# Expert weights loaded as pairs: one transfer of 2 MB instead of two of 1 MB, in a two-layer encoder with a top-2-of-8 expert layer

## The reference, cut to what matters

```python
def moe_swiglu(h, w_router, w_gate, w_up, w_down):
    logits = (h @ w_router).astype(jnp.float32)
    top_vals, top_idx = lax.top_k(logits, TOP_K)
    ...
    for e in range(N_EXPERTS):
        y = y + combine[..., e:e + 1] * swiglu(h, w_gate[e], w_up[e], w_down[e])
    return y
```

## Time and profile before

| | us |
|---|---|
| median of 3 runs | 1521.4 (1521.32 to 1521.8) |
| the profiled execution, its own time | 1522.17 |
| its span, first to last instruction | 1520.2 |
| TensorE busy in the span | 1500.5 |
| VectorE busy | 1190.6 |
| ScalarE busy | 1012.3 |
| granted TensorE clock, share of full speed | 0.999 |

### The profile page before, as it was taken

The page is one execution under the profiler, slowest core; times in us unless marked ns, Lnnn a source line. Parts: engine busy times, 40 slices in busy tenths (PEclk is TensorE's granted clock), DMA queues, the critical chain, the costliest instruction groups (busy, mean ns, idle before and its releaser), DMA issues.

```text
span 1520.2 us, 17780 instructions
## 1 busy us (share of the span) xinstructions
PE 1500.5 (99%) x7138; PEld 1248.9 (82%) x7138; DVE 1190.6 (78%) x960; ACT 1012.3 (67%) x971; POOL 52.5 (3%) x63
## 2 busy tenths in 40 slices
PE   9999999999999999999999999999999999999997
PEld 7888788888888888888888888888888888888885
DVE  5756755556566769899888888889889889899896
ACT  6555544435465577777777777777777777777774
POOL 1000000000000036000000000000000000000100
PEclk9999999999999999999999999999999999999999
DMA  9832555545642549999999999999999999999992
GB/s 350 337 124 91 187 194 193 180 152 173 205 163 91 172 167 424 407 347 415 372 363 400 376 374 384 392 374 372 392 380 368 391 377 373 397 365 368 420 402 92
DMA packets 96487, 460.03 MB, mean 303 GB/s; under 512 B 7656, under 2 KB 13304, under 8 KB 53392
## 3 DMA queue, kind: packets, MB, share of 16 engines
q1 hardware_dynamic: 91632, 444.58, 77.5%
q10 hardware_dynamic: 3312, 9.46, 1.7%
q0 software_dynamic: 1456, 4.79, 0.8%
HBM read 447.79 MB, written 11.01 MB: 302 GB/s over the span
## 4 chain that ended last, share of the span: by engine, by line
PE 94%; DVE 2%; ACT 1%; issue 1%; DMA 1%; SPq 0%; ACTq 0%; DVEq 0%
PE A L430 20%; PE A L432 20%; PE A L431 20%; PE DN L430 8%; PE DN L432 8%; PE DN L431 8%; PE T L1791 2%; PE DN L1586 1%; DMA xs<-in_x 1%; PE T L430 1%; PE T L431 1%; PE T L432 1%; PE A L1562 1%; DVE wlo L405 1%; PE T L1571 1%
## 5 line engine op out<-in xcount | busy, mean ns | idle before, releaser
L405 DVE TENSOR_TENSOR wlo<-raw,whi 128x2048 fp32r<-128x2048 f32 (+2 forms) x335 | 753.8, 2260 | 160.1 <-ACT whi L398 159.8
L398 ACT ACTIVATE whi<-raw 128x2048 fp32r<-128x2048 f32 (+2 forms) x335 | 632.5, 1895 | 215.8 <-PE A L432 121.1
L430 PE MATMUL A<-whi,heTh 128*128 128x512 f32 x672 | 266.3, 396 | 0.6 <-DVE heTl L1314 0.6
L432 PE MATMUL A<-whi,heTl 128*128 128x512 f32 x672 | 262.2, 390 | 0.0
L431 PE MATMUL A<-wlo,heTh 128*128 128x512 f32 x672 | 261.8, 390 | 0.0
L405 DVE TENSOR_TENSOR wlo_more<-raw,whi_more 128x2048 fp32r<-128x2048 f32 x84 | 192.2, 2288 | 38.1 <-ACT whi_more L398 38.1
L398 ACT ACTIVATE whi_more<-raw 128x2048 fp32r<-128x2048 f32 x84 | 161.1, 1918 | 36.4 <-PE A L432 18.4
L430 PE MATMUL A<-whi,hTh 128*128 128x512 f32 (+2 forms) x448 | 174.5, 389 | 4.8 <-DVE hTl L947 1.8
L431 PE MATMUL A<-wlo,hTh 128*128 128x512 f32 (+2 forms) x448 | 169.9, 379 | 0.0
L432 PE MATMUL A<-whi,hTl 128*128 128x512 f32 (+2 forms) x448 | 169.9, 379 | 0.0
L430 PE MATMUL DN<-whi,aTh 128*128 128x512 f32 x376 | 148.2, 394 | 1.1 <-DVE aTl L1333 1.1
(11 more groups left out here) (318 smaller groups left out, 1735.0 us busy)
## 6 DMA issues: line engine op xcount, KB each, us to landing
raw<-in_moe_w_gate SPq DMA_DIRECT2D x112, 1024.0 KB, 7.4
raw<-in_moe_w_up SPq DMA_DIRECT2D x112, 1024.0 KB, 7.5
raw<-in_moe_w_down SPq DMA_DIRECT2D x112, 1024.0 KB, 7.5
raw<-in_w_in SPq DMA_DIRECT2D x22, 1024.0 KB, 7.1
raw<-in_dense_w_down SPq DMA_DIRECT2D x11, 1024.0 KB, 4.9
raw<-in_dense_w_gate SPq DMA_DIRECT2D x10, 1024.0 KB, 5.1
raw<-in_dense_w_up SPq DMA_DIRECT2D x10, 1024.0 KB, 5.2
raw<-in_w_out SPq DMA_DIRECT2D x8, 1024.0 KB, 5.1
```

What stands on the lines that cost most here:

```text
L398: nc.scalar.activation(split_slot(u, e)[0][:, :n], raw[:, u % R, :n], ACT.Copy).then_inc(hi_done, 1)
L405: nc.vector.tensor_tensor(lo[:, :n], raw[:, u % R, :n], hi[:, :n].bitcast(F32), ALU.subtract).then_inc(lo_done, 1)
L430: nc.tensor.matmul(o, hi, wh, start=start, stop=False)
L432: return nc.tensor.matmul(o, lo, wh, start=False, stop=stop)
```

## The change

The host's layout and the number of bytes stay as they are. SP now issues one transfer for two neighbouring expert units, 2 MB, into two neighbouring raw slots. It waits until the second of the two slots is free (`u - R + 2` in place of `u - R + 1`). There are three such double slots in the six raw slots. Both units of a pair are told of by the landing semaphore of the first. The slots are numbered from `UM`, so that a pair never wraps around the end of `raw`; the units before the experts move by this to other slots, but each still follows the unit six before it.

```diff
+        def raw_slot(u):
+            return (u - UM) % R
+
+        def landed_with(u):
+            return u - (u - UM) % 2 if u >= UM else u
...
         def split_hi(act, u, e=None):
-            act.wait_ge(raw_landed[u % R], 16 * (u // R + 1) + times(e, 16 * EU // R))
+            v = landed_with(u)
+            act.wait_ge(raw_landed[v % R], 16 * (v // R + 1) + times(e, 16 * EU // R))
...
-            nc.scalar.activation(split_slot(u, e)[0][:, :n], raw[:, u % R, :n], ACT.Copy).then_inc(hi_done, 1)
+            nc.scalar.activation(split_slot(u, e)[0][:, :n], raw[:, raw_slot(u), :n], ACT.Copy).then_inc(hi_done, 1)
...
-            def load(u, dst_u, src, kt, n, e=None):
+            def load(u, src, kt, n):
                 if u >= R:
-                    sp.wait_ge(lo_done, u - R + 1 + times(e, EU))
-                sp.dma_start(raw[:, dst_u, :kt * n].rearrange("p (k n) -> p k n", k=kt), src
-                             ).then_inc(raw_landed[dst_u], 16)
+                    sp.wait_ge(lo_done, u - R + 1)
+                sp.dma_start(raw[:, raw_slot(u), :kt * n].rearrange("p (k n) -> p k n", k=kt), src
+                             ).then_inc(raw_landed[u % R], 16)
+
+            def load_two(u, src, kt, e):
+                sp.wait_ge(lo_done, u - R + 2 + times(e, EU))
+                i = raw_slot(u)
+                sp.dma_start(raw[:, i:i + 2, :].rearrange("p s (k n) -> p s k n", k=kt), src
+                             ).then_inc(raw_landed[u % R], 16)
...
-                def take(src, kt, n):
+                def take(src, kt):
                     nonlocal i
-                    load(base + i, (base + i) % R, src, kt, n, e)
-                    i += 1
+                    load_two(base + i, src, kt, e)
+                    i += 2
                 for j in range(EG + 1):
                     if j < EG:
                         for w in (gate, up):
-                            take(w[:, 2 * j], 4, N)
-                            take(w[:, 2 * j + 1], 4, N)
+                            take(w[:, 2 * j:2 * j + 2], 4)
                     if j:
-                        take(dn[:, 2 * j - 2], 2, D)
-                        take(dn[:, 2 * j - 1], 2, D)
+                        take(dn[:, 2 * j - 2:2 * j], 2)
```

More of the change, by code:

```diff
@@ L404, in split_lo @@
             hi, lo = split_slot(u, e)
-            nc.vector.tensor_tensor(lo[:, :n], raw[:, u % R, :n], hi[:, :n].bitcast(F32), ALU.subtract
+            nc.vector.tensor_tensor(lo[:, :n], raw[:, raw_slot(u), :n], hi[:, :n].bitcast(F32), ALU.subtract
                                     ).then_inc(lo_done, 1)
@@ L473, in load_half @@
             def load_half(u, src, n, half, landed):
-                sp.dma_start(raw[:, u, half * 2 * n:(half + 1) * 2 * n].rearrange("p (k n) -> p k n", k=2),
+                sp.dma_start(raw[:, raw_slot(u), half * 2 * n:(half + 1) * 2 * n].rearrange("p (k n) -> p k n", k=2),
                              src[:, 2 * half:2 * half + 2, :]).then_inc(landed, 16)
@@ L499, in _ @@
                 else:
-                    load(u, u % R, src, kt, n)
+                    load(u, src, kt, n)
                 if u == 2:
@@ L585, in first_high @@
                 c = slice(half * 2 * N, (half + 1) * 2 * N)
-                nc.scalar.activation(whi[:, u, c], raw[:, u, c], ACT.Copy).then_inc(signal, 1)
+                nc.scalar.activation(whi[:, u, c], raw[:, raw_slot(u), c], ACT.Copy).then_inc(signal, 1)
             act.dma_start(gcol[:], gain_columns).then_inc(gain_landed, 16)
@@ L932, in first_low @@
                 c = slice(half * 2 * N, (half + 1) * 2 * N)
-                nc.vector.tensor_tensor(wlo[:, u, c], raw[:, u, c], whi[:, u, c].bitcast(F32), ALU.subtract
+                nc.vector.tensor_tensor(wlo[:, u, c], raw[:, raw_slot(u), c], whi[:, u, c].bitcast(F32), ALU.subtract
                                         ).then_inc(signal, 1)
```

## The result

The change made the kernel slower: 1538.09 us (median of 4 runs, 1534.21 to 1540.75) against 1521.47 (1521.32 to 1521.8), a ratio of 1.0106 with a 95% interval of 1.0093 to 1.0118. The profiled execution took 1537.76 us with a span of 1536.0. The forecast was 1522.5, and its range ended at 1528.

The account below looks back on a forecast made before the run. PE was taken as the bound, transfers close behind. Experts 1 to 6 cost 0, the start of the experts 0.7, the last expert 0.4: +1.1 us, from 1521.4 to 1522.5, range 1520.8 to 1524.4, eight in ten 1520.6 to 1528.

Parts of the forecast that it names:

- What bounds the kernel: Whole span: PE is the bound, busy 1500.5 of 1520.2 us, with transfers only close behind.
- rival B: Experts: transfers were the bound, so 168 fewer would speed them up; 1520.8 us at best; chance 0.04.
- The odd unit is requested when it was before. The queue serves in order, so it lands about when it did: Experts: only the even unit is requested later, about 2.8 us; a pair lands in 7.4 us.
- The DMA has 11% to spare: Experts: the kernel needs 374 GB/s, while the engines moved 422 GB/s with always something queued.
- One pass in place of a loop: Experts 1 to 6, 126 pairs: splits late by up to 0.7 us, at least 3 us of cushion left, cost nothing.
- The two stretches: Start of the experts costs 0.7 us (0 to 2.2), the last expert 0.4 us (0 to 3).
- rival A: First and last expert starved: 2.2 and 3 us lost, late steps 1 to 2 more; about 1528 us; chance 0.14.
- the walks: Units around 10 and 308: landing to split, low part and PE's use, margins of 0.0 to 0.6 us.
- rival D: Every expert starved by pair landings of 10 us and more, six losing 1 to 2 us each; about 1531; chance 0.04.
- a landing median over 9 us: Experts: a sign named for a wrong forecast; 7.4 to 8 us at the median was the sign for right.
- Rival C: Expert transfers: paired form slow or on fewer engines; about 1626 us at 334 GB/s, some 2,330 at 200; chance 0.02.
- the 4.9 us in my bounds: Dense-layer loads: pieces of 2 KB more than 1 MB apart land in 4.9 us, so the 2 MB form costs nothing.

Follow-up runs that it names:

- x6: The changed kernel with half of the bytes in each expert transfer, the rest of each slot keeping old values; 1521.33 us, ratio 0.9998.
- x7: The changed kernel with a fourth double slot for the first seven experts, three again in the last; 1525.65 us, ratio 1.0028.
- x3_late_joint: The kernel of before, 1 MB transfers, both of a pair requested when the second slot is free, even unit split when both landed; 1533.89 us, ratio 1.0079.
- x1_late: The kernel of before, 1 MB transfers, only the even unit's request held back until the pair's second slot is free; 1521.87 us, ratio 0.9999.
- second traced one: The changed kernel run and traced once more, nothing altered; 1543.76 us, ratio 1.0124 to the kernel of before.
- x4_half_lo: The changed kernel with DVE taking the low part of half of each expert unit's columns, which PE reads twice; 1518.83 us, ratio 0.9980.

## Why the prediction was wrong, step by step

**What bounds the kernel: right.** x6 and x7 stay at PE's pace, and rival B, transfers as the bound of before, had nothing to give.

**"The odd unit is requested when it was before. The queue serves in order, so it lands about when it did": this step failed.** In experts 1 to 6 the odd unit landed 7.3 us after its request before, 9.9 after the change, and 9.4 and 9.7 in x3_late_joint and x1_late. The even unit had had a head start of 2.8 us, a little more than the 2.5 us of its transfer. Held back, it stands in front of the odd unit. I had allowed for that by adding 2.5 to the 4.9 us of a transfer alone, and found 7.4, the same number as the trace's median, by accident: the trace's 7.4 had a wait behind earlier requests in it that my sum left out. The quiet pairs landed in 7.5 us, so the sum was right for an empty queue and wrong for this one. The queue was never empty: each of the 126 pairs of experts 1 to 6 was requested while the pair before it had still to land, by 4.2 us at the median (from issues and landings of the trace). With half of the bytes (x6_half_bytes) that was 0.2 us, and the landing 5.2, the time of a quiet pair of that size.

**"The DMA has 11% to spare": it stands, but it is no promise for the landing time.** A mean seems to say otherwise. Queue 1 in mid-experts, and in the stretch with a long backlog that I had used, both of the kernel before (packets, MB, share of 16 engines):

```profile
q1 hardware_dynamic: 34680, 252.53, 95.9%
...
q1 hardware_dynamic: 2020, 14.72, 88.0%
```

252.53 MB in 680 us x 95.9% are 387 GB/s while busy; 14.72 MB in 40 us x 88.0% are 418. Against the 374 needed, mid-experts would leave 3%. But single slices of 17 us in the same 680 us, with all queues together, reach 422 to 425:

```profile
GB/s 402 397 369 377 373 318 422 407 391 376 377 373 318 425 397 401 372 375 378 313 425 398 392 379 374 375 312 424 409 392 376 376 372 325 424 406 385 368 377 370
```

And in the changed kernel 26 pairs of experts 1 to 6 were requested with more than 5 us of the one before still to come; they landed 4.98 us behind it at the median, which is 421 GB/s. So the transfers can go faster than the 5.6 us that PE takes for a pair. Requests come unevenly, though (nine in ten of them 4.4 to 7.5 us after the one before), and one that comes early waits in the queue. That this unevenness is why room of 11% goes with landings of 9.9 us fits the traces, but no run here changes it alone.

**One pass in place of a loop.** I set the odd unit's old landing against the even unit's old split, pair by pair, and found 3 us of cushion. But a late split releases its slot late, and the next request starts from there. A cushion is used up once; a loop that is 0.1 us too long comes round 56 times. In this simple form that would be 5.6 us spread evenly. The measured loss is larger and uneven, and single landings scatter around the median (7.5 to 12.5 us in experts 1 to 6), which fits. The sum that was needed is landing plus time to release, against the time PE gives it: 9.9 + 7.0 against 16.8. With my 7.4 it would have been 14.4, and still "nothing", so the landing time is the first error.

**The two stretches.** I gave the first expert 0.7 us and the last 0.4, with a top of 2.2 and 3. They lost 5.4 and 4.8, two thirds of the loss in this execution (2.0 and 7.9 in the second traced one). The kind was right, `aTl` behind the late split among it, and so were the two places of rival A, to which it gave 6.7 us in all; the walks assumed that the landings were pushed by 1.3 us and that nothing carried over. With four double slots the first expert lost nothing, and the last one, with three, still 4.3: there, too, it is the loop.

**The other 6.0 us**, in experts 1 to 6, are rival D: "landings of pairs of 10 us and more instead of 7.4". I gave it 0.04. It is the mechanism by which these six experts lose, and what I had named as a sign of being wrong, a landing median over 9 us, is what came.

**Rival C** and the power-of-two spacing: small at most. The first pair, alone, landed in 7.5 us; at the estimated 334 GB/s it would have been 2.4 + 6.3 = 8.7. One reading behind this was mixed up: the 4.9 us in my bounds are those of the dense `down` weights, in pieces of 4 KB from blocks 0.5 MB apart; the gate and up weights, in pieces of 2 KB from blocks 1.4 MB apart, landed in 5.1 and 5.2. The conclusion stays. The rule of the Trainium skill on power-of-two row pitches ("DMA: Bandwidth & Descriptors", section on latency and other measured facts) does not show in this load of pieces of 8 KB with 1 MB between the two of a partition.

## What to carry to other kernels

Before slots are bound together, add up the loop: request to landing with the queue as full as it will be, plus first use to release of the last one in the group, and hold it against what the bounding engine gives n groups. Binding k slots takes k - 1 units from the loop's time and adds k - 1 units to the landing, and larger transfers give nothing back where several small ones already overlap. Well below the edge it costs nothing, as with five single slots or one half of the change alone. Leave more room than the medians ask for: landings scatter, and with a sum of 16.7 against 16.8 us some of the loss was still there. A test with a sixteenth less work tells an edge from a cost in proportion, but not which resource makes the edge; for that, shorten another part of the loop or add a slot.

## What the runs showed of the hardware

The DMA engines' busy share did not tell how much more they could move: in the kernel of before it was 0.98 at 381 GB/s (700 to 1380 us) and 1.02 at 422 GB/s (1400 to 1440 us), and x4_half_lo kept PE fed at 377 GB/s with a share of 0.96. A kernel bound by such a loop also varies from run to run, 1536 to 1545 us for one program in one job, where the kernel of before, bound by PE, stayed within 0.8 us. And where PE had idle gaps its clock could come into the sum: one execution of the changed kernel had a mean granted clock of 0.995, and the one with triple slots 0.977, against 0.999.
